# A float32 transformer kernel on one core: the compression's four weight chunks put between the halves of two neighbouring groups

## The reference

```
kv = h @ kv_w                      # 1024 x 1536: keys and values of three branches (cmp, slc, win)
# compression, for keys and for values: overlapping blocks of 32 tokens, stride 16, flattened to 2048
hid = gelu((blocks + pos) @ cmp_w1)   # 2048 x 256
k_cmp, v_cmp = hid @ cmp_w2           # 256 x 64
```

## Time and profile before

| | |
|---|---|
| median of 3 runs (2092.24 to 2099.08) | 2094.92 us |
| profiled execution, its own time | 2092.86 us |
| its span | 2091.1 us |
| TensorE, matmul | 2051.6 us busy, 98% of the span |
| VectorE | 1545.2 us, 74% |
| ScalarE | 1043.7 us, 50% |
| GpSimd | 223.8 us, 11% |
| TensorE in 550 to 560 us | 8.90 of 10.00 us busy |
| TensorE in 520 to 550 us | 29.99 of 30.00 us busy |

### The profile page before, as it was taken

One profiled execution on the slowest core, in us unless ns is written; L12 is line 12 of the kernel. 1 busy time (PEld: TensorE's weight loads), 2 busy tenths in 40 slices (PEclk: granted clock), 3 DMA queues, 4 the chain that ended last, 5 costly groups with the idle time before them and its releaser, 6 DMA issues.

```text
span 2091.1 us, 39168 instructions
## 1 busy us (share of the span) xinstructions
PE 2051.6 (98%) x16828; PEld 2006.8 (96%) x16828; DVE 1545.2 (74%) x1932; ACT 1043.7 (50%) x1212; POOL 223.8 (11%) x352
## 2 busy tenths in 40 slices
PE   8999999999999999999999999999999999999998
PEld 8999999999999997999999999999998999999998
DVE  7788889888778889789885457677798455767554
ACT  6544646345643467553464453355456354346443
POOL 1111101111411110111110000011111000001000
PEclk9999999999999999999999999999999999999999
DMA  9898656995799940499845555458986455545663
GB/s 349 302 349 310 222 207 221 361 365 198 242 335 371 351 143 34 135 313 341 311 162 185 188 182 169 162 195 307 372 327 204 164 193 189 168 162 175 219 221 112
DMA packets 265550, 497.39 MB, mean 238 GB/s; under 512 B 17185, under 2 KB 146593, under 8 KB 265122
## 3 DMA queue, kind: packets, MB, share of 16 engines
q1 hardware_dynamic: 230354, 366.42, 51.6%
q0 software_dynamic: 35024, 128.47, 16.3%
HBM read 491.16 MB, written 1.05 MB: 235 GB/s over the span
## 4 chain that ended last, share of the span: by engine, by line
PE 84%; DVE 9%; ACT 4%; DMA 2%; issue 1%; POOL 0%; DVEq 0%; SPq 0%; ACTq 0%
PE PY L580 8%; PE PY L582 8%; PE PY L581 8%; PE PB L580 8%; PE PA L580 8%; PE PB L582 8%; PE PB L581 8%; PE PA L582 8%; PE PA L581 8%; DVE wlo L1690 2%; ACT whi L1201 1%; PE PA L620 1%; PE PB L620 1%; PE PY L613 1%; PE PB L613 1%
## 5 line engine op out<-in xcount | busy, mean ns | idle before, releaser
L1690 DVE TENSOR_TENSOR wlo<-raw,whi 128x2048 fp32r<-128x2048 f32 x327 | 750.3, 2303 | 319.4 <-ACT whi L1201 318.2
L1201 ACT ACTIVATE whi<-raw 128x2048 fp32r<-128x2048 f32 x321 | 612.4, 1912 | 481.5 <-DMA raw<-ffn_w_in 195.8
L580 PE MATMUL PY<-opB_hi,whi 128*128 128x256 f32 x1344 | 377.8, 281 | 6.6 <-DVE wlo L1690 6.6
L582 PE MATMUL PY<-opB_hi,wlo 128*128 128x256 f32 x1344 | 375.1, 279 | 0.0
L581 PE MATMUL PY<-opB_lo,whi 128*128 128x256 f32 x1344 | 375.0, 279 | 0.0
L580 PE MATMUL PA<-opA_hi,whi 128*128 128x256 f32 x1120 | 317.5, 283 | 4.9 <-DVE wlo L1690 4.2
L582 PE MATMUL PA<-opA_hi,wlo 128*128 128x256 f32 x1120 | 316.5, 283 | 0.0
L581 PE MATMUL PA<-opA_lo,whi 128*128 128x256 f32 x1120 | 315.6, 282 | 0.0
L580 PE MATMUL PB<-opA_hi,whi 128*128 128x256 f32 x1024 | 289.0, 282 | 1.9 <-DVE wlo L1690 1.9
L582 PE MATMUL PB<-opA_hi,wlo 128*128 128x256 f32 x1024 | 288.1, 281 | 0.0
L581 PE MATMUL PB<-opA_lo,whi 128*128 128x256 f32 x1024 | 287.2, 280 | 0.0
(11 more groups left out here) (387 smaller groups left out, 3938.5 us busy)
## 6 DMA issues: line engine op xcount, KB each, us to landing
raw<-ffn_w_in SPq DMA_DIRECT2D x176, 512.0 KB, 6.4
scr<-adat POOLq DMA_DIRECT2D x160, 512.0 KB, 6.4
raw<-w_in SPq DMA_DIRECT2D x144, 512.0 KB, 4.4
raw<-w_ff SPq DMA_DIRECT2D x128, 512.0 KB, 4.7
raw<-ffn_w_out SPq DMA_DIRECT2D x88, 512.0 KB, 5.3
adaw<-adat POOLq DMA_DIRECT2D x80, 512.0 KB, 6.6
raw<-w_branch SPq DMA_DIRECT2D x48, 512.0 KB, 4.6
raw<-a_w_in SPq DMA_DIRECT2D x24, 512.0 KB, 4.6
```

What stands on the lines that cost most here:

```text
L580: nc.tensor.matmul(o_, w1, rhs(xh), start=start, stop=False, skip_group_check=True)
L582: return nc.tensor.matmul(o_, w2_, rhs(xh), start=False, stop=stop, skip_group_check=True)
L1201: AC(whi[slot][:, 0:w], raw[slot][:, 0:w], ACT.Copy).then_inc(hi_ready, 1)
L1690: TT(wlo[slot][:, 0:w], raw[slot][:, 0:w], whi[slot][:, 0:w].bitcast(F32), ALU.subtract).then_inc(lo_ready, 1)
```

## The change

The four compression chunks no longer stand together. They are put between the halves of the third key-and-value group and of ffn10's group 0: third group's first half (c+4), compression 0 (c+5), second half (c+6), compression 1 (c+7), ffn10's first chunk (c+8), compression 2 (c+9), ffn10's second chunk (c+10), compression 3 (c+11). The 8 transposes follow. The total number of chunks and of products is the same. `hidden_turned` and `compressed_kv` move from ffn10's group 0 to its group 1. ScalarE's and VectorE's `prep_to` places are moved to fit. The core of the diff:

```diff
+KV2_AT = [CH["kv"] + 4, CH["kv"] + 6]
+CMP_AT = [CH["kv"] + 5, CH["kv"] + 7, CH["kv"] + 9, CH["kv"] + 11]
+IN0_AT = [CH["kv"] + 8, CH["kv"] + 10]
...
# SyncE
+            chunk(KV2_AT[0], src_in512(I["kv_w"], 1024, 0))
             need(sp, "S", "kv0")
             for u in range(2):
                 sp.dma_start(kvs[64 * u:64 * u + 64], kvc[64 - 64 * u:128 - 64 * u]).then_inc(kv_swapped, 16)
+            chunk(CMP_AT[0], src_in256(I["cmp_w1"][0], 0, 0))
+            chunk(KV2_AT[1], src_in512(I["kv_w"], 1024, 1))
+            chunk(CMP_AT[1], src_in256(I["cmp_w1"][0], 0, 8))
+            for h in range(2):
+                chunk(IN0_AT[h], src_ffn_in(I["ffn_w_in"][1, 0], 0, h))
+                chunk(CMP_AT[2 + h], src_in256(I["cmp_w1"][1], 0, 8 * h))
...
# TensorE; blocks(i) is the old loop body for one compression chunk
             for n_ in "AB":
                 take(n_)
-            zgroup(CH["kv"] + 4, "AB", tile_in512, "kv")
+            for h in range(2):
+                zchunk(KV2_AT[h], zbanks("AB"), tile_in512, range(4 * h, 4 * h + 4), "kv")
+                if h == 0:
+                    take("Y")
+                    need(pe, "V", "elo")
+                blocks(h)
             for n_ in "AB":
                 by(n_, "V", "kv2.z")
+            take("A")
+            for h in range(2):
+                chunk(IN0_AT[h], IN0_AT[h] % RING, PS["A"], tile_ffn_in, range(4 * h, 4 * h + 4), 4, "C", 0, 7, lo_of("10"))
+                blocks(2 + h)
...
# TensorE, in ffn: the two closures run at group 1
-                            if between and j == 0:
+                            if between and j == 1:
                                 between[h]()
...
# ScalarE
             for hf in range(2):
                 split_high(kvc, hf, hf)
-            prep_to(c + 6)
             act.wait_ge(cmp_in, 64)
             S(AC(eh[:, :, 512:528], pos2, ACT.Copy), "epos")
             act.wait_ge(kv_swapped, 32)
             for hf in range(2):
                 split_high(kvs, hf, 1 - hf)
+            prep_to(c + 6)
+            zcopy("kv1", [kslc[:, 0, :], kslc[:, 1, :], vtmp["slc"][:, 0, :], vtmp["slc"][:, 1, :]])
             prep_to(c + 7)
-            zcopy("kv1", [kslc[:, 0, :], kslc[:, 1, :], vtmp["slc"][:, 0, :], vtmp["slc"][:, 1, :]])
             for k in range(4):
                 high10(k)
             prep_to(c + 8)
             for k in range(4, KT):
                 high10(k)
-            prep_to(c + 9)
+            prep_to(c + 10)
             zcopy("kv2", [kwin[:, 0, :], kwin[:, 1, :], vtmp["win"][:, 0, :], vtmp["win"][:, 1, :]])
-            prep_to(c + 11)
...
# VectorE
             for hf in range(2):
                 split_low(kvc, hf, hf)
-            prep_to(c + 6)
             need(dve, "S", "epos")
...
             for hf in range(2):
                 split_low(kvs, hf, 1 - hf)
+            prep_to(c + 6)
             need(dve, "S", "kv0")
             dve.wait_ge(multiplied, c + 4)
             zevac("kv1", "Y")
...
+            prep_to(c + 9)
             need(dve, "S", "kv1")
-            dve.wait_ge(multiplied, c + 6)
+            dve.wait_ge(multiplied, KV2_AT[1] + 1)
             zevac("kv2", "AB")
-            prep_to(c + 12)
+            prep_to(c + 13)
```

More of the change, by code:

```diff
@@ L488, in ffn @@
                         sp.dma_start(posi.bitcast(I32), I["positions"].partition_broadcast(P)).then_inc(b2_in, 16)
+                    if name == "ffn10" and (kind, j) == ("in", 0):
+                        continue
                     if kind == "in":
@@ L510, in _ @@
             ffn("ffn01", I["ffn_w_in"][0, 1], I["ffn_w_out"][0, 1])
-            for g in range(3):
+            for g in range(2):
                 for h in range(2):
                     chunk(CH["kv"] + 2 * g + h, src_in512(I["kv_w"], 512 * g, h))
+            chunk(KV2_AT[0], src_in512(I["kv_w"], 1024, 0))
             need(sp, "S", "kv0")
@@ L517, in _ @@
                 sp.dma_start(kvs[64 * u:64 * u + 64], kvc[64 - 64 * u:128 - 64 * u]).then_inc(kv_swapped, 16)
-            for kv in range(2):
-                for h in range(2):
-                    chunk(CH["cmp"] + 2 * kv + h, src_in256(I["cmp_w1"][kv], 0, 8 * h))
+            chunk(CMP_AT[0], src_in256(I["cmp_w1"][0], 0, 0))
[4 more added lines that the diff above has]
+                chunk(CMP_AT[2 + h], src_in256(I["cmp_w1"][1], 0, 8 * h))
             ffn("ffn10", I["ffn_w_in"][1, 0], I["ffn_w_out"][1, 0])
@@ L688, in ffn @@
                         buf = "AB"[j % 2]
-                        take(buf)
                         for h in range(2):
+                            if between and j == 0:
+                                continue
+                            if h == 0:
+                                take(buf)
                             chunk(p_ + h, (p_ + h) % RING, PS[buf], tile_ffn_in, range(4 * h, 4 * h + 4), 4, op, 0, 7,
-                                  lo_of(tag) if j == (2 if z else 0) else None)
-                            if between and j == 0:
+                                  lo_of(tag) if z and j == 2 else None)
+                            if between and j == 1:
                                 between[h]()
@@ L838, in _, with blocks @@
             zpair(CH["kv"], "kv", ("kv0", "kv1"))
+            def blocks(i):
+                c = CMP_AT[i]
+                kv, h, slot = i // 2, i % 2, c % RING
+                pe.wait_ge(lo_ready, c + 1)
+                o_ = flat["Y"][0:65, 512 * kv:512 * kv + 256]
+                for k in range(8):
+                    kk = 8 * h + k
+                    wh, wl = whi[slot][:, 256 * k:256 * k + 256], wlo[slot][:, 256 * k:256 * k + 256]
+                    xh, xl = (e_[:, kv, kk:kk + 513:8] for e_ in (eh, el))
+                    nc.tensor.matmul(o_, xh, wh, start=kk == 0, stop=False, skip_group_check=True)
+                    nc.tensor.matmul(o_, xh, wl, start=False, stop=False, skip_group_check=True)
+                    last = nc.tensor.matmul(o_, xl, wh, start=False, stop=kk == 15, skip_group_check=True)
+                last.then_inc(multiplied, 1)
@@ L1308, in ffn @@
                     prep_to(p_ + 4)
-                    if name == "ffn10" and j == 0:
+                    if name == "ffn10" and j == 1:
                         need(act, "V", "pbias")
@@ L1516, in _ @@
                 high10(k)
-            prep_to(c + 9)
+            prep_to(c + 10)
             zcopy("kv2", [kwin[:, 0, :], kwin[:, 1, :], vtmp["win"][:, 0, :], vtmp["win"][:, 1, :]])
-            prep_to(c + 11)
             for kv in range(2):
-                act.wait_ge(multiplied, CH["cmp"] + 2 * kv + 2)
+                act.wait_ge(multiplied, CMP_AT[2 * kv + 1] + 1)
                 S(AC(hraw[0:65, 256 * kv:256 * kv + 256], flat["Y"][0:65, 512 * kv:512 * kv + 256], ACT.Copy), f"hraw{kv}")
                 if kv == 0:
-                    prep_to(c + 12)
+                    prep_to(c + 14)
             need(act, "T", "vtrans")
@@ L1892, in ffn @@
                             need(dve, "S", "csil1")
-                        if j == 0 and name == "ffn10":
+                        if j == 1 and name == "ffn10":
                             need(dve, "T", "hidt")
```

## The result

The changed kernel took 2113.15 us (median of 6 runs, 2103.25 to 2118.00), the kernel before 2095.86 in the same session. The ratio is 1.0080, 95% interval 1.0065 to 1.0095: **slower by 17 us, where +5.3 was forecast** and the range ended at 2104.5. Four further executions of the same changed kernel in a later session had a median of 2105.25 (2103.25 to 2115.18; the kernel before 2094.68), ratio 1.0063 (1.0042 to 1.0085). The profiled execution took 2118.00, the slowest of the six.

What follows compares the result with a forecast made beforehand. TensorE was taken to bound the kernel, busy for 98% of the span. Stops added 6.69 us, removed waits saved 1.65, small products added 0.2: +5.2 us, 2100.2 us; range 2096.0 to 2104.5 with rivals and scatter.

Steps and rivals of the forecast that it cites:

- the two stops in front: New TensorE stops at compression chunk 0 and the third group's second half: 3.72 and 2.75 us, plus 0.11 each.
- Stop 1: At compression chunk 0, due 540.59: late transfer, then evacuation of PY behind VectorE's split; 3.72 us plus 0.11.
- Rival B: Chunk 0 lands later still, beside the next transfer: up to 1.5 us more, 2101.7 us; sign: landing after 539.5; chance 0.12.
- C: Rival: no new stop, only the two old ones gone, 2093.3 us; chance 0.04.
- D: Rival: only one of the two new stops is paid, +2.4 us, 2097.3 us; chance 0.1.
- stop 2: At the third group's second half (c+6), due 547.45: ScalarE's high part behind the late kv1 copy; 2.75 us plus 0.11.
- Rival A: TensorE's clock falls after chunk 0's stop; free during chunk 0, +1.65 us if low in c+6, 2101.9 us; chance 0.25.
- the sum of these terms: Both new stops less the removed waits, without the small products: 6.69 us added, 1.65 removed.
- the small products' cover: At compressed_kv, GELU ready T + 12.3, wanted T + 12.63: 0.3 us of cover; cost 0.2 us, bounds nothing to 1.0.
- the prediction's own sign of too thin a cover: A stop at compressed_kv above 0.5 us would mean the small products' cover is thinner than worked out.
- the rule of exclusion: VectorE two-input and GpSimd SBUF-reading instructions exclude each other: sum 1.0 us larger by the rule, 0.1 by the trace.
- The removed waits: TensorE's two old waits at line 857, before the third and fourth compression chunks, go: 1.00 and 0.65 us, together -1.65.

Runs made afterwards that it cites:

- e3: Changed kernel with VectorE's zevac("kv1") put ahead of prep_to(c + 6): 2105.5 us, ratio to the kernel before 1.0056.
- r6: Changed kernel with compression chunk 0 asked for before SyncE's wait for kv0: 2106.81 us, ratio to the kernel before 1.0061.
- e2: Changed kernel with ffn10's first six conditioning transfers issued early, right behind acc_x("kv"): 2098.6 us, ratio to the kernel before 1.0020.
- e4: Kernel before, chunks in the old order, with only the small products, GELU, pbias and VectorE's copies moved one group later: 2102.6 us.
- r9: Changed kernel, chunk 0 asked for before the kv0 wait, prep_to(c + 6) and prep_to(c + 7) at old places, GELU and pbias behind group 0's SiLU: ratio 1.0005.
- r10: Changed kernel with zevac("kv1") ahead of prep_to(c + 6) on VectorE, GELU and pbias behind group 0's SiLU and product: ratio to the kernel before 1.0020.
- r5: Changed kernel run again without any edit: median 2105.25 us, ratio to the kernel before 1.0063.
- r7: Changed kernel, chunk 0 asked for before the kv0 wait, prep_to(c + 6) and prep_to(c + 7) at old places, six conditioning transfers early: 2101.15 us.

## Why the prediction was wrong

**Right: the two stops in front and their mechanism.** Both are where they were put. Stop 1 was 4.04 between starts (541.83 to 545.87) against 3.72: the landing took 7.1 us from the issue and not 6.8, the split 2.50 and not 2.40. e3 and r6 confirm the chain: evacuation behind the split, copy behind the evacuation, c+6 behind the copy. Rival B is out: chunk 0 landed at 540.15, past the 539.5 that was to tell it, but TensorE runs 1.24 us later in this profile from the first boundary on, so 0.3 us is left, not 1.5. C and D are out.

**Right: what a low clock does there.** The granted clock did fall behind stop 1:

```profile
545.00:546.00 1.00, 0.14 (x1) 0.14 (x2) 0.81 (x2) 0.15 (x1) 0.00 (x0) 0.62 1.06 345
546.00:547.00 1.00, 1.00 (x5) 1.00 (x6) 0.00 (x0) 1.00 (x3) 0.00 (x0) 0.50 1.10 353
```

Chunk 0 took 4.20 us and not 3.14, and stop 2 shrank to 1.67 from the 2.75 forecast. The sum of the three is that of the forecast within 0.3 us: the loss fell into the next stop. Rival A had this, and its costly case, a low clock in c+6, did not come.

**Right in size: the sum of these terms.** Had the third stop not come, TensorE would have begun ffn10's group 2 near 591.3 (590.4 for the last product of group 1, 0.84 for the small products), 6.5 after the 584.83 of the kernel before, or 5.2 with the offset of 1.24 taken off. The forecast has 5.0 for them. e2, in which the third stop is gone, measured about 4.8 over the whole stretch.

**The step that failed: the small products' cover.** The prediction said: "Bounds: nothing, up to 1.0 if a transfer lands as late as T + 7.5. I take 0.2", and "The conditioning work of this FFN starts on a chunk count, not on time, and moves with TensorE; nothing waits for it at its head." T is 577.84 in the changed kernel. c+15 landed at T + 14.7, and the stop was 7.2 us in place of 0.2; the prediction's own sign of too thin a cover was 0.5. The chain behind the landing was worked out rightly (high 1.9, split 2.3, `pbias`, GELU 0.9 with little between); its starting point was wrong. The prediction took the data of c+14 and c+15 as there when ScalarE came to them, one right behind the other after the SiLU. c+15 is ffn10's chunk c0 + 5 (c0 is CH["ffn10"], c+10); the GELU of the kernel before stands behind c0 + 3, which is on time. The trace of before had c0 + 5's landing, and GpSimd's burst ahead of it:

```profile
567.08 1.13 POOL L2422 DMA_DIRECT2D adaw<-adat  x2 [20.90 <-PE PA L582]
568.20 1.04 POOL L2422 DMA_DIRECT2D scr<-adat  x2
573.03 1.05 POOL L2422 DMA_DIRECT2D scr<-adat  x2 [3.79 <-PE PA L582]
```

```profile
577.89 1.92 ACT L1201 ACTIVATE whi<-raw 128x2048 fp32r<-128x2048 f32 x1 [4.13 <-DMA raw<-ffn_w_in]
...
584.25 1.91 ACT L1201 ACTIVATE whi<-raw 128x2048 fp32r<-128x2048 f32 x1 [3.93 <-DMA raw<-ffn_w_in]
```

The second of these ScalarE rows is c0 + 5: issued at 572.77, landed 11.5 us later. It holds the longest landing of the earlier trace rows, 11.1 us for one of its halves; the prediction took only their median, 5.0. Today nothing is late for it; a GELU put behind it would have been done at 584.25 + 5.3 = 589.6, 5.7 us after `compressed_kv` wants it. e4 measured 5.3. The moved instruction should have been costed against the landing of the chunk that it moves behind. The prediction also left out VectorE's copies out of PY, which move with the small products; in the changed kernel the third stop hides that, in r9 and r10 it cost 1.4 and 1.6 us.

**The second part of the miss: the price of the long stop's clock.** Rival A was priced for the first two stops alone. Behind the third the clock was at 1.2 GHz from about 593 to 603.4:

```profile
598.00:600.00 2.00, 2.00 (x22) 1.69 (x23) 0.31 (x1) 1.99 (x3) 0.00 (x0) 0.50 0.00 0
600.00:602.00 2.00, 2.00 (x11) 2.00 (x11) 0.88 (x2) 2.00 (x3) 0.00 (x0) 0.50 0.03 8
```

TensorE worked through 5.6 us of it, so 2.8 were lost. 5.2 + 7.3 + 2.8 = 15.3; the stretch cost 15.4 in r5 and 17.0 in the first profile, whose list has 1.3 us more at line 589 in ffn10.

**A mean that hid a wait.** The prediction took GpSimd's eight `tensor_scalar` as 1.0 us each, the mean, and set the rule of exclusion that it cites against the split's 2.40 us. In the trace of before they took from 0.55 to 3.09 us, with a median of 0.76. The two splits that overlap them took 2.40 and 2.61 us, against 2.29 alone: 0.1 and 0.3 us more, less than one such instruction. The one of 3.09 us is as long as the shortest and a whole split together. So these rows do not speak against the rule; the mean of eight did not show what one instruction takes. The forecast's 2.40 stands; it was 2.50 in the changed kernel.

**The removed waits** did go: none stands ahead of compression chunks 2 and 3. They were worth 1.65 us at most.

**Open:** why the first session's six runs lie mostly at 2111 to 2118. The profile shows low clock at more of the kernel's ordinary waits behind the stretch (30.8 us of it; 10.3 in the kernel before), but r5 with the same program had 3.4. Whether the change makes them likelier was not settled.

## What to carry to other kernels

When an instruction moves behind a prefetched chunk on its engine, it inherits that chunk's landing; look that landing up in the trace, also where nothing waits for it now. Ask as well who reads the result and frees the buffer: that reader moves too. A burst of transfers that is hidden has a place where it is hidden, and both moving it and moving work under it need the slack of each transfer beside it. A stop right in front of another stop is partly free, the clock's fall included; a long stop ahead of dense work costs its length and the half clock behind it.

## What the runs showed of the hardware

A chunk of 1 MB landed 7 us after its issue when only a swap of 0.5 MB stood ahead of it (chunk 0), and 14 to 15 us after it beside six transfers of GpSimd's queue (c+15 in the changed kernel, chunk 0 in r7). The Trainium skill (DMA: Bandwidth & Descriptors, "Issuing engines are not separate DMA queues") says that transfers issued by different engines run on the same DMA engines and interleave; the two landings agree with it.

Two executions of one program with the same three stops in the changed stretch differed by 14.3 us, and the time with low granted clock by 27.3 us (47.8 and 20.5). At half speed 27.3 us would cost up to 13.7, by an estimate.

Beside a VectorE split of 2.3 us, one GpSimd `tensor_scalar` took 3.09 us where the shortest took 0.55.
